# Delta rule: the transposed triangular inverse taken by transposes of the inverse, in place of an update by its own product

## The reference, cut to what matters

```
lower = where(strict, beta[:, None] * (k @ k.T) * decay, 0)
sol   = triangular_solve(lower, concat([v * beta, k * beta * exp(g)]), unit_diagonal=True)
u, w  = split(sol)
for each chunk:  v_new = u - w @ S;  o = q_dec @ S + qk @ v_new;  S = S * g_last + k_dec.T @ v_new
```

## Time and profile before

| what | us |
|---|---|
| median of 3 runs (lowest, highest) | 1775.28 (1773.97, 1776.09) |
| the profiled execution's own time | 1773.64 |
| its span, first to last instruction | 1771.5 |
| TensorE busy | 1679.3 (95%) |
| VectorE, ScalarE, GpSimd busy | 875.3, 783.6, 201.5 |

### The profile page before, as it was taken

How to read it: one execution, slowest core, us unless ns; L and a number is a source line. 1 busy time by engine, 2 the same in 40 slices (tenths; PEclk the granted TensorE clock), 3 DMA queues, 4 the chain that set the end, 5 groups by cost and what they waited for, 6 DMA issues and landing times.

```text
span 1771.5 us, 21811 instructions
## 1 busy us (share of the span) xinstructions
PE 1679.3 (95%) x8436; PEld 1334.6 (75%) x8436; DVE 875.3 (49%) x1388; ACT 783.6 (44%) x1345; POOL 201.5 (11%) x233
## 2 busy tenths in 40 slices
PE   6899999999988899999999799999997999999998
PEld 4678888888877687677777588777675888888867
DVE  4746556556554535455555543544336532344346
ACT  3533543543543424565665622555544432243243
POOL 0111211111102200023232300000002000000011
PEclk9899999999999999999999999999998999999999
DMA  4111111111110322322222122211121333233321
GB/s 167 60 36 36 60 48 37 60 49 36 60 37 24 111 96 84 114 78 72 78 70 69 36 96 95 68 50 58 48 72 48 107 100 100 90 103 101 102 72 48
DMA packets 40165, 127.29 MB, mean 72 GB/s; under 512 B 4576, under 2 KB 9104, under 8 KB 40064
## 3 DMA queue, kind: packets, MB, share of 16 engines
q1 hardware_dynamic: 38112, 121.65, 20.8%
q0 software_dynamic: 1040, 3.27, 0.5%
q10 hardware_dynamic: 912, 0.99, 0.2%
HBM read 122.69 MB, written 2.15 MB: 70 GB/s over the span
## 4 chain that ended last, share of the span: by engine, by line
PE 83%; DVE 7%; ACT 6%; issue 3%; POOL 1%; DMA 0%; SPq 0%; ACTq 0%; DVEq 0%
PE ps L637 81%; ACT L L1521 3%; DVE wl L1713 2%; DVE L L2162 1%; PE ps L975 1%; PE ps L783 1%; DVE qkv L1749 1%; POOL h L2409 1%; ACT wh L1126 1%; DVE qb L1800 0%; ACT L L1473 0%; DMA wraw<-in_wa 0%; DVE mo L2285 0%; ACT xr L1390 0%; DVE U L2026 0%
## 5 line engine op out<-in xcount | busy, mean ns | idle before, releaser
L637 PE MATMUL ps<-xr,wh 128*128 128x512 f32 x2752 | 906.9, 411 | 15.5 <-DVE wl L1713 14.1
L637 PEld LDWEIGHTS ps<-xr,wh 128*128 128x128 f32 x2752 | 502.7, 190 | 139.6 <-issue 36.5
L637 PE MATMUL ps<-xr,wl 128*128 128x512 f32 x1376 | 542.1, 394 | 0.0
L1713 DVE TENSOR_TENSOR wl<-wraw,wh 128x1024 fp32r<-128x1024 f32 x214 | 261.3, 1235 | 153.3 <-ACT wh L1126 151.8
L637 PEld LDWEIGHTS ps<-xr,wl 128*128 128x128 f32 x1376 | 260.4, 189 | 57.3
L1126 ACT ACTIVATE wh<-wraw 128x1024 fp32r<-128x1024 f32 x214 | 220.3, 1047 | 20.3 <-PE ps L637 17.8
L637 PE MATMUL ps<-xm,wh 128*128 128x512 f32 x640 | 200.8, 395 | 12.8 <-DVE xm L2278 8.6
L637 PEld LDWEIGHTS ps<-xm,wh 128*128 128x128 f32 x640 | 120.2, 189 | 44.2 <-issue 9.8
L637 PE MATMUL ps<-xm,wl 128*128 128x512 f32 x320 | 125.3, 392 | 0.0
L2394 POOL TENSOR_SCALAR L<-L,m 128x256 f32<-128x256 f32 (+1 forms) x128 | 75.6, 611 | 325.5 <-DVE m L2177 325.5
L2338 POOL TENSOR_TENSOR Mm<-AT,masks 128x512 f32<-128x512 f32 x56 | 82.8, 1485 | 239.3 <-PE ps L637 122.8
(11 more groups left out here) (240 smaller groups left out, 1946.5 us busy)
## 6 DMA issues: line engine op xcount, KB each, us to landing
wraw<-in_wa SPq DMA_DIRECT2D x48, 512.0 KB, 3.3
wraw<-in_wb SPq DMA_DIRECT2D x32, 512.0 KB, 3.3
wraw<-in_wu SPq DMA_DIRECT2D x32, 512.0 KB, 3.3
wraw<-in_wd SPq DMA_DIRECT2D x32, 512.0 KB, 3.3
wraw<-in_wao SPq DMA_DIRECT2D x16, 512.0 KB, 3.4
wraw<-in_wbo SPq DMA_DIRECT2D x16, 512.0 KB, 3.3
wraw<-in_wc SPq DMA_DIRECT2D x16, 512.0 KB, 3.3
bias<-rel_rows SPq DMA_DIRECT2D x16, 256.0 KB, 3.7
```

Source lines behind the costliest of these rows:

```text
L637: return e.matmul(out, w, x, start=start, stop=stop, skip_group_check=True)
L1713: e.tensor_tensor(m.wl[:, i % N_SPLIT, :], m.raw[:, i % N_RAW, :], m.wh[:, i % N_SPLIT, :].bitcast(F), ALU.subtract).then_inc(s.wlo, 1)
```

## The change

T is no longer updated by its own product. After levels 0 to 4, where the diagonal blocks of U reach at most 32 rows, VectorE transposes U into T in 32x32 blocks right after U is written. After level 5 (blocks of 64 rows) TensorE transposes U into PSUM in a turn of its own, and ScalarE copies it to T. The call that transposed U0 on TensorE is gone, and its yield stays. The order of calls, counts of semaphores and waits on reuse are renumbered (22 calls per head on TensorE, not 27); prep has 29 yields, not 28.

```diff
-STEPS = {"gates": 5, "prep": 28, ...
+STEPS = {"gates": 5, "prep": 29, ...
-PREP_P = 27
+PREP_P = 22
+PREP_LEVEL = {1: 8, 2: 10, 3: 12, 4: 14, 5: 16, 6: 19}
...
 # TensorE
-        o = begin(8)
-        e.wait_ge(s.prep_v, prep_v(h, "U0"))
-        end(8, turn4(o, lambda n: U[:, n, :]), (s.prep_a, prep_a(h, "T")))
-        yield
-        call = 9
-        for i in range(1, 7):
+        yield
+        for i, call in PREP_LEVEL.items():
             o = begin(call)
-            if i == 1:
-                e.wait_ge(s.prep_a, prep_a(h, "T"))
+            if i == 6:
+                e.wait_ge(s.prep_a, prep_a(h, "T5"))
             else:
                 e.wait_ge(s.prep_v, prep_v(h, f"T{i - 1}"))
             e.wait_ge(s.prep_o, prep_o(h, f"M{i}"))
             end(call, four(o, lambda n: m.Mm[:, i % 2, n, :], lambda n: m.Tm[:, n, :]), (s.prep_a, prep_a(h, f"P{i}")))
-            call += 1
-            yield
-            if i < 6:
-                o = begin(call)
-                e.wait_ge(s.prep_a, prep_a(h, f"P{i}"))
-                e.wait_ge(s.prep_v, prep_v(h, f"U{i - 1}"))
-                end(call, four(o, lambda n: U[:, n, :], lambda n: m.Pm[:, n, :]), (s.prep_v, prep_v(h, f"T{i}")))
-                call += 1
-            o = begin(call)
+            yield
+            o = begin(call + 1)
             e.wait_ge(s.prep_a, prep_a(h, f"P{i}"))
-            e.wait_ge(s.prep_v, prep_v(h, f"U{i - 1}"))
-            end(call, four(o, lambda n: m.Pm[:, n, :], lambda n: U[:, n, :]), (s.prep_v, prep_v(h, f"U{i}")))
-            call += 1
-            yield
+            end(call + 1, four(o, lambda n: m.Pm[:, n, :], lambda n: U[:, n, :]), (s.prep_v, prep_v(h, f"U{i}")))
+            yield
+            if i == 5:
+                o = begin(call + 2)
+                e.wait_ge(s.prep_v, prep_v(h, "U5"))
+                end(call + 2, turn4(o, lambda n: U[:, n, :]), (s.prep_a, prep_a(h, "T5")))
+                yield
...
 # ScalarE: no copy of T ahead of level 1
+            if i == 5:
+                did(e.activation(m.Tm[:], product(call + 2)[1], ACT.Copy))
+                yield
...
 # VectorE
+        def turn_squares(i):
+            after(f"U{i}")
+            did(e.transpose(m.Tm[:].rearrange("p n c -> p (n c)"), U.rearrange("p n c -> p (n c)")))
...
         did(e.tensor_tensor(U, m.ident.unsqueeze(1).to_broadcast([128, 4, 128]), m.Mm[:, 0], ALU.subtract))
+        if h:
+            e.wait_ge(s.prep_p, prep_p(h - 1, 19))
+        turn_squares(0)
...
-            if i < 6:
-                o = product(call)
-                e.wait_ge(s.prep_a, prep_a(h, "T"))
-                if i > 1:
-                    after(f"T{i - 1}")
-                did(e.tensor_tensor(m.Tm[:], m.Tm[:], o, ALU.subtract))
-                call += 1
-            o = product(call)
+            o = product(call + 1)
             after(f"U{i - 1}")
             did(e.tensor_tensor(U, U, o, ALU.subtract))
+            if i < 5:
+                turn_squares(i)
+            yield
+            if i == 5:
+                yield
```

More of the change, by code:

```diff
@@ L192 @@
 FILL = {1: 0.95, HEADS: 0.7, HEADS + 1: 4}
-STEPS = {"gates": 5, "prep": 28, "recur": 10, "kv_post": 4, "attend": 9, "attend2": 9, "split_o": 1, "split_ob": 1,
+STEPS = {"gates": 5, "prep": 29, "recur": 10, "kv_post": 4, "attend": 9, "attend2": 9, "split_o": 1, "split_ob": 1,
          "stick0": 12, "stick1": 14, "ple": 8}
@@ L563, in __init__ @@
         self.gs, self.gm, self.go = new("gate_sigmoid"), new("gate_times"), new("gate_out")
-PREP_P = 27
+PREP_P = 22
+PREP_LEVEL = {1: 8, 2: 10, 3: 12, 4: 14, 5: 16, 6: 19}
 PREP_A = {n: i + 1 for i, n in enumerate(
-    ("silu0", "silu1", "sq0", "sq1", "silu2", "silu3", "eb", "ln0", "ex0", "ln1", "ex1", "E", "v0", "v1", "T",
-     "P1", "P2", "P3", "P4", "P5", "P6", "w"))}
+    ("silu0", "silu1", "sq0", "sq1", "silu2", "silu3", "eb", "ln0", "ex0", "ln1", "ex1", "E", "v0", "v1", "P1",
+     "P2", "P3", "P4", "P5", "T5", "P6", "w"))}
 PREP_V = {n: i + 1 for i, n in enumerate(
-    ("dv", "y0", "y1", "qdn", "at", "qk", "kg", "kd", "U0", "T1", "U1", "T2", "U2", "T3", "U3", "T4", "U4", "T5", "U5",
+    ("dv", "y0", "y1", "qdn", "at", "qk", "kg", "kd", "U0", "T0", "U1", "T1", "U2", "T2", "U3", "T3", "U4", "T4", "U5",
      "U6"))}
@@ L826, in prep @@
             end(call, four(o, lambda n: m.Mm[:, i % 2, n, :], lambda n: m.Tm[:, n, :]), (s.prep_a, prep_a(h, f"P{i}")))
-            call += 1
             yield
-            if i < 6:
-                o = begin(call)
-                e.wait_ge(s.prep_a, prep_a(h, f"P{i}"))
-                e.wait_ge(s.prep_v, prep_v(h, f"U{i - 1}"))
-                end(call, four(o, lambda n: U[:, n, :], lambda n: m.Pm[:, n, :]), (s.prep_v, prep_v(h, f"T{i}")))
-                call += 1
-            o = begin(call)
+            o = begin(call + 1)
             e.wait_ge(s.prep_a, prep_a(h, f"P{i}"))
-            e.wait_ge(s.prep_v, prep_v(h, f"U{i - 1}"))
-            end(call, four(o, lambda n: m.Pm[:, n, :], lambda n: U[:, n, :]), (s.prep_v, prep_v(h, f"U{i}")))
-            call += 1
+            end(call + 1, four(o, lambda n: m.Pm[:, n, :], lambda n: U[:, n, :]), (s.prep_v, prep_v(h, f"U{i}")))
             yield
-        o = begin(call)
+            if i == 5:
[3 more added lines that the diff above has]
+                yield
+        o = begin(21)
         e.wait_ge(s.prep_v, prep_v(h, "U6"))
-        end(call, four(o, lambda n: m.kg[:, n, :], lambda n: U[:, n, :]), (s.prep_a, prep_a(h, "w")))
+        end(21, four(o, lambda n: m.kg[:, n, :], lambda n: U[:, n, :]), (s.prep_a, prep_a(h, "w")))
         yield
@@ L1329, in prep @@
             yield
[L1330 to L1333, removed]
         yield
-        call = 9
-        for i in range(1, 7):
+        for i, call in PREP_LEVEL.items():
             o = product(call)[1]
             if i > 1:
-                e.wait_ge(s.prep_p, prep_p(h, call - 1))
+                e.wait_ge(s.prep_p, prep_p(h, PREP_LEVEL[i - 1] + 1))
             elif h:
-                e.wait_ge(s.prep_p, prep_p(h - 1, 25))
+                e.wait_ge(s.prep_p, prep_p(h - 1, 20))
             did(e.activation(m.Pm[:], o, ACT.Copy))
@@ L1344, in prep @@
             yield
-            call += 3 if i < 6 else 2
-        o = product(call)[1]
+            if i == 5:
+                did(e.activation(m.Tm[:], product(call + 2)[1], ACT.Copy))
+                yield
+        o = product(21)[1]
         if h >= 2:
@@ L2002, in prep @@
         if h:
-            e.wait_ge(s.prep_p, prep_p(h - 1, 26))
+            e.wait_ge(s.prep_p, prep_p(h - 1, 21))
         if h == 0:
@@ L2010, in prep @@
         did(e.tensor_tensor(U, m.ident.unsqueeze(1).to_broadcast([128, 4, 128]), m.Mm[:, 0], ALU.subtract))
+        if h:
+            e.wait_ge(s.prep_p, prep_p(h - 1, 19))
+        turn_squares(0)
         yield
-        yield from idle(3)
-        call = 9
-        for i in range(1, 7):
+        yield
+        yield
+        yield
+        for i, call in PREP_LEVEL.items():
             yield
-            call += 1
-            if i < 6:
-                o = product(call)
-                e.wait_ge(s.prep_a, prep_a(h, "T"))
-                if i > 1:
-                    after(f"T{i - 1}")
-                did(e.tensor_tensor(m.Tm[:], m.Tm[:], o, ALU.subtract))
-                call += 1
-            o = product(call)
+            o = product(call + 1)
             after(f"U{i - 1}")
             did(e.tensor_tensor(U, U, o, ALU.subtract))
-            call += 1
+            if i < 5:
+                turn_squares(i)
             yield
+            if i == 5:
+                yield
         yield
@@ L2348, in prep @@
         else:
-            e.wait_ge(s.prep_p, prep_p(h - 1, 24))
+            e.wait_ge(s.prep_p, prep_p(h - 1, 19))
         e.wait_ge(s.prep_v, prep_v(h, "at"))
@@ L2353, in prep @@
         yield from idle(6)
-        call = 9
-        for i in range(1, 7):
+        for i, call in PREP_LEVEL.items():
             if i < 6:
[L2357 to L2360, removed]
+                e.wait_ge(s.prep_v, prep_v(h, "U0"))
+                if i > 1:
+                    e.wait_ge(s.prep_p, prep_p(h, PREP_LEVEL[i - 1]))
                 level(i + 1)
-            call += 3
             yield
             yield
+            if i == 5:
+                yield
         yield
```

## The result

The change makes the kernel slower: 1788.09 us median (1787.16 to 1789.98, 4 runs) against 1774.82 (1773.97 to 1776.09, 4 runs), ratio 1.0077 with interval [1.0066, 1.0089], 13.3 us. The forecast was 1776.0, its range ended at 1787. The profiled execution after took 1788.59, its span is 1786.8.

What follows compares the result with a forecast made beforehand. TensorE, busy 95% of the span, was taken as the bound. Ends cost 2.3 + 1.85, middle rounds gain 3.4: +0.7 on 1773.64 gives 1774.4, stated as a 1776.0 median; range 1769 to 1787 us.

Steps and rivals of the forecast that it cites:

- clock 1.00 there: Expected sign in head 7's bare end: TensorE's granted clock stays at the full level, 1.00.
- rival 4: TensorE's clock falls in head 7's bare end, 7 us on top, 1783 us; chance 0.06.
- The transpose: VectorE's 128x512 transpose after levels 0 to 4, taken as 0.69 us, like the kernel's other 128x512 operations.
- The estimate of 0.71: Alternative transpose time worked out from a skill figure of 311 ns for 128x128 bf16; sum 0.5 us larger.
- The waits of a middle round: TensorE idle before P2 1.03, P3 none, P4 1.06, P5 1.18, and the late TensorE transpose 0.30 us.
- Rivals 1 to 3: Cheap transpose, 1769 to 1773 (chance 0.17); dear, over 0.83 us (0.20); no waits, 37 us gained, 1738 (0.02).
- TensorE's busy time in a round: Expected sign in each middle round: TensorE's busy time falls by about 4.5 us.
- The gain of a middle round: Each preparation of heads 1 to 6 gets 0.57 us shorter, 3.4 us for six.
- The bare levels: Unfilled levels take 4.55 us instead of 3.82; from P5 to P6 5.25, which is 1.43 more.
- Head 7's chain: Last preparation, nothing left to fill with: P6 and w come 2.3 us late.
- Head 0's: First preparation: P2 about 0.1 us early, P6 and w 1.85 us late.
- The forecast's reason: Whole kernel: 37 us of TensorE work traded for uncovered VectorE steps on the same chain.

Runs made afterwards that it cites:

- e1: The changed kernel with dummy TensorE products put into the gaps of heads 0 and 7; 1781.51 us, ratio to before 1.0036.
- e4: The changed kernel with each VectorE transpose of heads 1 to 6 done twice; 1806.54 us, ratio to before 1.0168.
- e9: New form in heads 1 to 6, old in 0 and 7, projection steps of rounds 2 to 7 placed by VectorE's queue; 1752.63 us, ratio to before 0.9873.
- e5: The changed kernel with projection steps of rounds 2 to 7 moved toward TensorE's waits; 1799.22 us, ratio to before 1.0125.
- e7: New form in heads 1 to 6, old in 0 and 7, projection steps moved toward the waits as in e5; 1784.96 us, ratio to before 1.0049.
- e3: Old form in heads 1 to 6, new form in heads 0 and 7; 1790.29 us, ratio to before 1.0088.
- e11: The changed kernel, all eight heads with the transposes, projection steps dealt by the table of e9; 1770.17 us, ratio to before 0.9966.

## Why the prediction was wrong

**The step that failed is the clock in the bare ends.** The prediction says "clock 1.00 there", and has a fall as rival 4, at a chance of 0.06, for head 7 alone, as "nine groups of 0.81 at half speed 7 us come on top: 1783". It fell in both ends, and e1 puts the fall at 6 to 10 of the 12.1 us by which the forecast was short. The rows had shown 1.00 with gaps of 0.73 and 0.50 after 4.05; the forecast set the new gaps of up to 1.8 on the side of the first, on no row. Head 0 was left out of it although its own working makes the same chain of waits there. The Trainium skill ("TensorE: Matmul & The Clock Gate", A second HAM failure mode: psum-queue depth-cycling) tells of a kernel in which frequent short idle times between groups of products made the clock oscillate. The trace after agrees in that the clock fell with no gap over 1.78 ahead of it, once in each end. The prediction drew on another sentence of that page and not on this one.

**The other terms, in the forecast's own order.**
- The transpose: 0.711 us against 0.69 taken. The estimate of 0.71 that the prediction worked out from a figure of the Trainium skill ("VectorE: DVE Perf Modes", The three transpose paths) agrees with the row.
- The waits of a middle round: 0.87, 0, 1.04, 1.25 and 0.17 against 1.03, 0, 1.06, 1.18 and 0.30. Right, and e4 shows that the transpose is on their path. Rivals 1 to 3 are out. TensorE's busy time in a round fell by 3.25, not by the 4.5 that the prediction names as a sign.
- The gain of a middle round: 0.13 against 0.57, so six give 0.8 and not 3.4. 0.24 of the missing 0.44 stands between U4 and P5 (3.78 against 3.54): a tap of 1.84 (233.37), 1.27 in the round before the change, delays U4's subtraction. GpSimd's mask product runs beside this tap for all of its 1.28 us (from 233.38); taps of the same round without one beside them take 0.71 to 0.75. The rest is a sum of pieces between -0.06 and 0.08 a step.
- The bare levels: 4.61 against 4.55, and 5.22 to 5.27 from P5 to P6 in e1, at full clock, against 5.25. Head 7's chain is 2.7 longer (P1 to w 28.55 in e1, 25.45 before, less the 0.44 by which P1 comes earlier), forecast 2.3. Head 0's is 2.8 (w at 114.89 in e1, at 111.22 before, less 0.9 by which this execution was already late ahead of the chain), forecast 1.85; it goes wrong at P2, 0.5 late there (91.89 against 90.50) instead of 0.1 early.

With these three sizes the sum is +4.7 in place of +0.7, and e1's span is 5.3 over before. The forecast's reason, 37 us of TensorE work traded for VectorE steps on the same chain that are not covered, is right, and e9 shows its other half: once covered, they are a gain.

## What to carry to other kernels

TensorE work that is taken out of a filled stage can be worth next to nothing until the filling is dealt out anew (here 0.13 us a round at first, and 2.5 with both kernels refilled), and a filling step has to be placed by all that it brings into the other engines' lists, not by its own products. A stretch in which a dependent chain already shows is the wrong place for a trade of TensorE work against latency: it pays the latency, and the thinner stream can cost the clock on top. Before a slower run is explained by its waits, the granted clock of the same stretch has to be read beside them: in e5 and e7 most of the loss was the clock's. Where two forms compete, try each stage with its own: here the old form in the two ends and the new one in between, refilled, is the fastest of the kernels run.

## What the runs showed of the hardware

- TensorE's clock went from 1.00 to 0.50 in a stream of groups with gaps of 0.78 to 1.78 us, with no standstill, and came back when the groups ran back to back (1.00 from 122 and from 586). It fell for some 4 us in filled rounds too, behind a gap of 2.19 (0.57 in e5, 224 to 228), at a cost of 1.6 us each time (e7).
- Neither the instructions nor the length of one gap fix the fall: with the same list for the end of head 0 it came at U5 after and only at w in e3, and in head 7 at P5 after and at U3 in e11; the gap of 2.19 was followed by a fall in five of the six refilled rounds of e7 and not in the first.
- Dummy products in the gaps alone kept it at 1.00 (e1): here more work took less time.
- A group of four float32 products with a projection step behind it holds TensorE 0.88 to 0.89 us where it starts after a wait and 0.80 to 0.81 where it follows other products, so a wait costs some 0.08 more than its length.
- A VectorE transpose of 128x512 in float32, from SBUF to SBUF in 32x32 blocks, takes 0.711 us, the same in all 40.
